# Turning the input rows on VectorE instead of TensorE, and two column groups of the query latent at once

## The reference, cut to what matters

```
h = rmsnorm(x) * norm_gain                    # over 4096 features
p = h @ w_in                                  # 4096 x about 14,000 columns
cq, ckv, kpe, mq, mk, mv, mo, mi, mf, za, zb = columns of p   # cq has 1536
y = x + [MLA(cq, ckv, kpe) * silu(za) ; mLSTM(mq, mk, mv, mo, mi, mf) * silu(zb)] @ w_out
```

## Time and profile before

| | us |
|---|---|
| median of 3 runs (lowest, highest) | 2008.21 (2006.99, 2009.09) |
| profiled execution | 2007.37 |
| its span | 2005.6 |
| TensorE busy in the span | 1996.1 |
| VectorE, ScalarE, GpSimd busy | 1191.9, 910.7, 192.3 |
| granted clock of TensorE, mean | 0.999 of full |

### The profile page before, as it was taken

How to read it: one execution, slowest core, us unless ns; L and a number is a source line. 1 busy time by engine, 2 the same in 40 slices (tenths; PEclk the granted TensorE clock), 3 DMA queues, 4 the chain that set the end, 5 groups by cost and what they waited for, 6 DMA issues and landing times.

```text
span 2005.6 us, 36262 instructions
## 1 busy us (share of the span) xinstructions
PE 1996.1 (100%) x14891; PEld 1972.6 (98%) x14891; DVE 1191.9 (59%) x2292; ACT 910.7 (45%) x1814; POOL 192.3 (10%) x228
## 2 busy tenths in 40 slices
PE   9999999999999999999999999999999999999998
PEld 9999999999999999999999999999999999999998
DVE  5545677776566576666765555444455665555544
ACT  5644456565444443334444444444444543333333
POOL 0011043434200000000000001000000000000000
PEclk9999999999999999999999999999999999999999
DMA  9655443333455454645546555555555566666665
GB/s 253 185 172 155 121 123 106 109 102 124 118 172 148 146 170 126 178 128 168 158 139 176 169 168 168 169 168 168 169 168 168 169 184 193 195 193 193 194 192 141
DMA packets 213821, 323.27 MB, mean 161 GB/s; under 512 B 25104, under 2 KB 89128, under 8 KB 213656
## 3 DMA queue, kind: packets, MB, share of 16 engines
q1 hardware_dynamic: 210408, 317.42, 54.8%
q10 hardware_dynamic: 3248, 3.54, 0.5%
HBM read 310.11 MB, written 9.62 MB: 159 GB/s over the span
## 4 chain that ended last, share of the span: by engine, by line
PE 99%; DMA 0%; DVE 0%; ACT 0%; issue 0%; ACTq 0%
PE bank L1769 30%; PE bank L1773 30%; PE bank L1772 30%; PE bank L2043 1%; PE bank L2013 1%; PE bank L1939 1%; PE bank L1942 1%; PE bank L1941 1%; PE bank L1794 0%; PE bank L2115 0%; PE bank L2141 0%; PE bank L2009 0%; PE bank L2010 0%; PE bank L2168 0%; PE bank L2153 0%; DMA con<-in_shape_table_dram 0%
## 5 line engine op out<-in xcount | busy, mean ns | idle before, releaser
L1154 DVE TENSOR_TENSOR wlo<-raw,whi 128x512 fp32r<-128x512 f32 (+1 forms) x1256 | 813.9, 658 | 744.4 <-ACT whi L753 739.5
L1769 PE MATMUL bank<-xsplit,whi 128*128 128x288 f32 (+2 forms) x4128 | 1221.1, 296 | 0.3 <-DVE wlo L1154 0.3
L1773 PE MATMUL bank<-xsplit,wlo 128*128 128x288 f32 (+2 forms) x4128 | 1213.3, 294 | 0.0
L1772 PE MATMUL bank<-xsplit,whi 128*128 128x288 f32 (+2 forms) x4128 | 1213.0, 294 | 0.0
L753 ACT CAST whi<-raw 128x512 fp32r<-128x512 f32 (+1 forms) x1256 | 707.1, 575 | 953.3 <-PE bank L1773 910.4
L1769 PEld LDWEIGHTS bank<-xsplit,whi 128*128 128x128 f32 (+1 forms) x4128 | 774.1, 188 | 3.3 <-DVE wlo L1154 1.2
L1772 PEld LDWEIGHTS bank<-xsplit,whi 128*128 128x128 f32 (+1 forms) x4128 | 774.1, 188 | 1.8 <-issue 1.0
L1773 PEld LDWEIGHTS bank<-xsplit,wlo 128*128 128x128 f32 (+1 forms) x4128 | 773.5, 187 | 0.0
L1769 PE MATMUL bank<-latents,whi 128*128 128x288 f32 (+1 forms) x352 | 112.8, 320 | 0.1
L1772 PE MATMUL bank<-latents,whi 128*128 128x288 f32 (+1 forms) x352 | 107.0, 304 | 0.0
L1773 PE MATMUL bank<-latents,wlo 128*128 128x288 f32 (+1 forms) x352 | 106.8, 303 | 0.0
(11 more groups left out here) (303 smaller groups left out, 1227.6 us busy)
## 6 DMA issues: line engine op xcount, KB each, us to landing
raw<-in_w_in_dram SPq DMA_DIRECT2D x313, 512.0 KB, 3.8
raw<-in_w_out_dram SPq DMA_DIRECT2D x128, 512.0 KB, 3.9
raw<-in_w_in_dram SPq DMA_DIRECT2D x146, 256.0 KB, 3.1
raw<-in_w_q_up_dram SPq DMA_DIRECT2D x48, 384.0 KB, 3.4
raw<-in_w_kv_up_dram SPq DMA_DIRECT2D x16, 512.0 KB, 3.7
xres<-in_x_prompt_dram SPq DMA_DIRECT2D x32, 128.0 KB, 3.8
out_dram<-ytok SPq DMA_DIRECT2D x28, 128.0 KB, 3.5
xt<-in_x_prompt_dram SPq DMA_DIRECT2D x7, 384.0 KB, 8.9
```

The source lines that it names most:

```text
L1154: ins = tt(lo, src, hi.bitcast(f32), ALU.subtract)
L1769: ins = mm(out, w_hi, m_hi, start=start, stop=False, **kw)
L1772: mm(out, w_hi, m_lo, start=False, stop=False, **kw)
L1773: return mm(out, w_lo, m_hi, start=False, stop=stop, **kw)
```

## The change

**x is loaded in another layout and turned by VectorE.** `xt` is now 4 quarters of 32 partitions; a quarter holds a quarter of the features of a chunk of k tiles, for all token rows, in 10 blocks of 32 rows (the first block: 16 zero rows and the 16 meta rows; 8 of the prompt; one of the sample). Chunks are of 2, 2, 4, 4, ... k tiles. VectorE's `transpose` turns every 32 by 32 square of [128, 10 x 32] at once, reading every second or fourth element. A k tile then holds the features m·p + j of its chunk on partition p, so the weight rows are loaded in that order (`w_rows`, `qk_rows`), and the gains are laid out so on the host. The loads of x are 4 DMAs of 32 partitions per chunk, with 512 B runs (256 B in the first two chunks); the sample and meta rows are 12 DMAs at chunk 0 and chunk 2.

**Two groups at once.** Groups 0 and 1 become one loop of 64 units: unit 2k is columns 0 to 511 of k tile k in banks 0 to 3, unit 2k + 1 columns 512 to 1023 in banks 4 to 7. A slot of `raw` holds the 1024 columns of one k tile in 4 KB runs. The third group is as before.

**Row sums.** Ten squares of [128, 1024], one at each step of the third group (12 at every second step before); one fp32 matmul of 304 columns in place of three. **Narrow units.** 18 DMAs in place of 8. **Tables.** The loads of the constants and of the cache move to the third group. **Warming.** 18 transposes in one go.

```diff
-X_BLOCKS = [(0, 256), (256, 512)] + [(a, a + 512) for a in range(512, D_MODEL, 512)]
+CHUNKS = [(0, 2), (2, 2)] + [(k, 4) for k in range(4, KT, 4)]
-WARM = (4, 9)
+WARM = 18
 @@ SyncE
+        def w_rows(k, n, cols):
+            k0, m = CHUNKS[chunk_of(k)]
+            return w_in[k0 * P:(k0 + m) * P, cols].rearrange("(p k) c -> p k c", k=m)[:, k - k0:k - k0 + n, :]
+        def x_rows(eng, b):
+            k0, m = CHUNKS[b]
+            w, at = SQUARE * m, SQUARE * k0
+            for a in range(4):
+                f = k0 * P + a * w
+                eng.dma_start(xt[SQUARE * a:SQUARE * a + SQUARE, 1:9, at:at + w],
+                              x_prompt[0, :, f:f + w].rearrange("(b r) e -> r b e", r=SQUARE)).then_inc(x_in[b], 16)
+        def x_end_rows(eng, b, n, rows, places):
...
+            for a in places:
+                eng.dma_start(xt[SQUARE * a + r0:SQUARE * a + SQUARE, block, at:at + n * w]
+                              .rearrange("r (n e) -> r n e", n=n), src[a]).then_inc(x_in[b], 16)
+            x_rows(sp, 0)
+            sp.wait_ge(eps_set, 2)
+            x_end_rows(sp, 0, 2, meta, (0, 1))
+            first_weights(0)
+            x_rows(sp, 1)
+            first_weights(1)
+            first_weights(2)
+            sp.wait_ge(eps_set, 3)
+            x_end_rows(sp, 2, len(CHUNKS) - 2, x_sample[0], range(4))
+            x_end_rows(sp, 2, len(CHUNKS) - 2, meta, range(4))
+            for k in range(3, KT):
+                if k % 4 == 3 and k < KT - 1:
+                    x_rows(sp, chunk_of(k + 1))
+                first_weights(k)
 @@ ScalarE
+        def first_groups(x_part, now, after):
+            for k in range(KT):
+                for u in (2 * k + AHEAD, 2 * k + AHEAD + 1):
+                    if u == 2 * k + AHEAD and k + X_AHEAD < KT:
+                        x_part(k + X_AHEAD)
+                    if u < 2 * KT:
+                        now(u)
+                    else:
+                        after(u - 2 * KT)
             def x_tile(k):
-                b = 4 + k % 4
-                act.wait_ge(full[b], use("x", b, k // 4) + 1)
-                nc.scalar.activation(xhi[:, k, :], bank[b][:, 0:NT], ACT.Copy,
+                act.wait_ge(x_turned, k + 1)
+                nc.scalar.activation(xhi[:, k, :], xs[:, k % 2, X_PAD:], ACT.Copy,
 @@ VectorE
+            def x_turn(k):
+                b = chunk_of(k)
+                k0, m = CHUNKS[b]
+                if k == k0:
+                    dve.wait_ge(x_in[b], 16 * X_PIECES[b])
+                if k >= 2:
+                    dve.wait_ge(xlo_d, k - 1)
+                at = SQUARE * k0
+                nc.vector.transpose(xs[:, k % 2, :].rearrange("p (b r) -> p b r", r=SQUARE),
+                                    xt[:, :, at + k - k0:at + SQUARE * m:m]).then_inc(x_turned, 1)
+            for k in range(KT):
+                if k + X_AHEAD < KT:
+                    x_turn(k + X_AHEAD)
+                for u in (2 * k + AHEAD, 2 * k + AHEAD + 1):
+                    if u < 2 * KT:
+                        two_units(u)
+                    else:
+                        cq_units(u - 2 * KT)
+                    if u == 2 * k + AHEAD and k + X_AHEAD < KT:
+                        x_rest(k + X_AHEAD)
 @@ TensorE
-            warm(WARM[0])
-            for k in range(X_AHEAD):
-                x_tile(k)
-            warm(WARM[1])
-            group(0, "cq", 0, 0, N_META, lambda k: x_tile(k + X_AHEAD) if k + X_AHEAD < KT else None, x_ready=True)
+            warm(WARM)
+            for k in range(KT):
+                pe.wait_ge(xlo_d, k + 1)
+                for half in range(2):
+                    u = 2 * k + half
+                    pe.wait_ge(lo_done, u + 1)
+                    for ct in range(4) if k else (0, 2, 1, 3):
+                        b, s = 4 * half + ct, slice(ct * P, ct * P + P)
+                        ins = mm3(bank[b][:, 0:NQ], ...)
...
-                    for t, (c0, n) in enumerate(X_TOK):
-                        ins = mm(bank[4][:, c0:c0 + n], ones[0:n, :], diag[0:n, c0:c0 + n], start=True, stop=True)
+                    mm(bank[4][:, 0:NT], ones, diag[:, X_PAD:], start=True, stop=True).then_inc(full[4], 1)
```

More of the change, by code:

```diff
@@ L161, in shape_constants @@
     part("gains")[:] = gain_columns(inputs)
-    part("perm")[0:112, :] = np.roll(np.eye(112, dtype=np.float32), N_META, axis=1)
+    part("squares")[:] = np.tile(np.eye(SQUARE, dtype=np.float32), (P // SQUARE, 1))
     for b in range(2):
@@ L197, in gain_columns @@
         t[:, at:at + len(rows)] = rows.T
+    rows = np.asarray(inputs["norm_gain"]).reshape(-1)
+    for k, m in CHUNKS:
+        t[:, G_X + k:G_X + k + m] = rows[k * P:(k + m) * P].reshape(P, m)
     for at, name in ((G_QR, "q_rope_norm"), (G_KR, "k_rope_norm")):
@@ L468, in load, with group @@
                 sp.dma_start(dst, src).then_inc(raw_in[slot], 16)
-            def group(b0, col, src=w_in_t, blocks=KT // 2, width=512, first=0, between=lambda n: None):
+            def group(b0, col, src=w_rows, blocks=KT // 2, width=512, first=0, between=lambda n: None):
                 for n in range(first, blocks):
@@ L516, in cache_rows @@
                 if n == 0:
-                    for b in range(4, 8):
-                        sp.wait_ge(full[b], use("cq", b))
+                    sp.wait_ge(xlo_d, KT)
                     sp.dma_start(cacher[:, 0:512], cache_ckv[0]).then_inc(cache_in, 16)
@@ L659, in _ @@
             for i in range(0, 8):
-                group(U_OUT // 2 + i * (KT // 2), i * 512, w_out_t, between=out_rows(i))
+                group(U_OUT // 2 + i * (KT // 2), i * 512, lambda k, n, cols: w_out_t[:, k:k + n, cols],
+                      between=out_rows(i))
             for half in range(2):
@@ L680, in hymba_step @@
         T_NAR = [4 * turns] * RAW_SLOTS
-        T_PAIR = [4 * turns + 2] * RAW_SLOTS
+        T_PAIR = [4 * turns + d for d in NAR_LOADS]
         T_ML = [t + MLA_HEADS // 2 * pair_turns for t in T_PAIR]
@@ L768, in x_tile, with cq_evict @@
                                      scale=G[:, G_X + k:G_X + k + 1]).then_inc(xhi_d, 1)
-            def cq_evict(i):
+            def cq_evict(phase, g, b0=0):
                 for ct in (0, 2):
[L773 to L777, removed]
-                    x_tile(k)
-                cq_units(0)(k)
@@ new lines, in cq_evict @@
+                    nc.scalar.copy(cqraw[:, ds(g * 4 + ct, 1), :], bank[b0 + ct][:, 0:NQ]).then_inc(free[b0 + ct], 1)
+            for k in range(X_AHEAD):
+                x_tile(k)
+                two_units(2 * k)
+                if 2 * k + 1 < AHEAD:
+                    two_units(2 * k + 1)
+            first_groups(x_tile, two_units, cq_units)
+            cq_evict("cq_two", 0)
+            cq_evict("cq_two", 1, 4)
+            def x_squares(k):
+                if k < X_ROWS:
+                    if k == 0:
+                        for b, pieces in enumerate(X_PIECES):
+                            act.wait_ge(x_in[b], 16 * pieces)
+                        act.wait_ge(eps_set, 3)
+                    else:
+                        act.wait_ge(xsq, k)
+                    nc.scalar.activation(junk[:, :], xt[:, k, :], ACT.Square, accum_out=xss[:, k:k + 1])\
+                        .then_inc(xsq, 1)
@@ L806, in _, with row_hooks, ckv_units @@
-            cq_evict(1)
-            steps(KT, cq_units(2), cq_units(3), row_rstd)
-            cq_evict(2)
+            def row_hooks(k):
+                x_squares(k)
+                row_rstd(k)
+            def ckv_units(k):
+                unit(U_CKV + k, k, landed(T_CKV, k))
+            steps(KT, cq_units, ckv_units, row_hooks)
+            cq_evict("cq", 2)
             def ckv_hooks(k):
@@ L829, in narrow_units @@
             def narrow_units(k):
-                unit(U_NAR + k, k, landed(T_NAR, k, 0, 2), 288)
+                unit(U_NAR + k, k, landed(T_NAR, k, 0, NAR_LOADS[k // 2]), 288)
             def pair_units(n):
@@ L835, in pair_units @@
                 return split
-            steps(KT, lambda k: unit(U_CKV + k, k, landed(T_CKV, k)), narrow_units, ckv_hooks)
+            steps(KT, ckv_units, narrow_units, ckv_hooks)
             def rstd(dst, src, scale, bank_no, used, done):
@@ new lines, in _ @@
+            for k in range(X_AHEAD):
+                x_turn(k)
+            for k in range(X_AHEAD):
+                x_rest(k)
+                two_units(2 * k)
+                if 2 * k + 1 < AHEAD:
+                    two_units(2 * k + 1)
+            for k in range(KT):
[8 more added lines that the diff above has]
+                        x_rest(k + X_AHEAD)
@@ L1189, in row_squares @@
+            cq_evict("cq_two", 0)
+            cq_evict("cq_two", 1, 4)
+            def row_squares(k):
+                if k == 11:
+                    dve.wait_ge(xsq, X_ROWS)
+                    for b in range(X_ROWS):
+                        ts_(diag[:, SQUARE * b:SQUARE * b + SQUARE], c("squares"), xss[:, b:b + 1], None,
```

(2 more changed lines are left out.)

224 lines of the change are left out of this document (93 added, 131 removed).

## The result

| us | before | after |
|---|---|---|
| median (lowest, highest; runs) | 2007.74 (2006.99, 2009.09; 4) | 2028.83 (2028.04, 2029.58; 4) |
| profiled execution, span | 2007.37, 2005.6 | 2029.58, 2027.8 |

The kernel got slower by 21.1 us: ratio 1.0107, 95% interval 1.0095 to 1.0119. The prediction said 2005.6 with a range to 2013.0; it was wrong.

A forecast was written before the change was run, and what follows sets the result against it. TensorE's work was taken to bound the kernel, with a VectorE-ScalarE chain pacing the double group: its end moves from 118.19 to 115.9 us, 2.3 saved, with row sums 2.6, giving 2005.6 us by the median; range 2000.0 to 2013.0.

The forecast's parts named there:

- row sums: On TensorE, one fp32 matmul of 304 columns replaces six records of 0.58 us: 0.3 us saved.
- TensorE's side: TensorE's list: 30 in-line x transposes gone, 9.2 us, plus row sums 0.3; worth 9.5 us if nothing else limited.
- what I cost at nothing: Squares, bank copies, ten more narrow-unit DMAs and weight row order: all hidden by leads and cover, so 0 us.
- the full slow turn: Turn at its upper end, 0.83 us: a double-group step of 3.60 us and 2014.5 us in all.
- I take 0.50, the nearest form in size and source.: VectorE's turn of 128 x 320 in the double group: 0.50 us, between bounds of 0.37 and 0.83.
- the chain: Double group: VectorE and ScalarE wait on each other, 3.27 us per k tile against TensorE's 3.12.
- the strided turn is slow: Rival: turn up to 0.83 us, step 3.60, 2014.5 us; slower than before beyond a 0.60 turn; chance 0.16.
- The other five terms: Double-group step besides the turn: ScalarE's start 0.03, x tile 0.43, cast 0.65, two VectorE rests 1.22, x rest 0.44.
- I take 19.3: Start: k tile 3's weights, behind 28 issues, issued near 15.4 us and landing at 19.3; VectorE waits 2.9 us.
- short runs are dear: Rival at the start: 256 and 512 B runs cost double, k tile 3 lands at 24.5, +5.2: 2010.8 us; chance 0.12.
- TensorE sets the pace: Rival in the double group: step under 3.12 us, group ends at 111.2, 7.3 us less, 2000.9; chance 0.17.

The follow-up runs named there:

- e1: Changed kernel with an unused 352-byte tile ahead of nraw, putting xsplit and the later tiles back at their old addresses: 2014.54 us, ratio 1.0037.
- e3: e1 with VectorE's turn reading 32 elements in a row instead of every fourth or second (wrong outputs, same cost): 2007.65 us, ratio 1.0002.
- e6: e5 with the sample and meta rows of chunks 3 to 9 loaded behind k tile 4's weights, in eight more DMAs: 2001.53 us, ratio 0.997.
- e5: e1 with each VectorE turn done a step earlier, in mid-step between a weight rest and the x rest: 2004.23 us, ratio 0.9985.
- e10: e1 with only the rows of x in xsplit moved 4 bytes later, from byte 62540 to 62544: 2044.58 us, ratio 1.0187.

## Why the prediction was wrong

Forecast -2.6, measured +21.1: 23.7 to explain. The runs give:

| term | us | from |
|---|---|---|
| place of the rows against the weights | 14.3 | after - e1, 2028.83 - 2014.54 (13.8 if each is taken against the kernel before measured beside it) |
| turn 0.745 in place of 0.50 | 7.0 | 27 steps x 0.26 (3.53 - 3.27); e1 - e3 measured 6.9 |
| weights of k tile 3 at 21.4, not 19.3 | 2.1 | the cast's row |
| sum | 23.4 | |

The last two terms can be seen at the start of the third group: 125.55 for 115.9 is 9.65 us, of which they make 9.1. The 0.3 us of the row sums was not measured by itself.

- *"TensorE's side"*, and "what I cost at nothing": the price of a matmul was taken as fixed, so that only a changed list could change TensorE's time. This failed, for 14.3 us of the 23.7. The table part of the change, smaller constants, was priced at nothing because no instruction went with it. No rival had it either. It carried the result far out of the range, but even without it, in e1, the time is 2014.5 and the range ended at 2013.0, short of the full slow turn that the prediction itself had priced at 2014.5.
- *"I take 0.50, the nearest form in size and source."* This is the failed term of the chain. The upper bound of 0.83 was the nearer end, and the rival *the strided turn is slow* came true: its point of decision was a turn of 0.60; with 0.745 its own sum is -2.6 + 27 x 0.26 = +4.4. The Trainium skill (SBUF — State Buffer, "Door 1: The DMA port swizzle") wants two hits for each 16-byte line for full bandwidth and gives 4 fp32 as the free step. The turns at step 2 (two hits a line, 0.50) agree; those at step 4 (one hit, 0.745: 22.9 us for all 32 turns, less four of 0.50, over 28) are not free: (745 - 500)/320 = 0.77 ns more an element. The measurement decides.
- The other five terms held within 0.02 us, and the step of e3 (3.29 against 3.27) confirms the sum. The turns start 0.61 after the start of a rest, as was said of turns that all start at partition 0.
- *"I take 19.3"* for k tile 3: the issue came 1.2 us earlier than computed (14.19 for 15.4: 0.48 us an issue, not 0.525), and the landing was later all the same, 7.2 us from issue to cast instead of 3.8. The row of issues was not what held it: e6 left the number of issues and took bytes and short runs away, and gained. In kind that is the rival *short runs are dear*, at 2.1 us of its 5.2; runs of 256 and 512 B are most of the packets there, and the comparison of e5 and e6 points to their length, but length and bytes were not varied apart. The clock's dip behind the wait (0.83 in the window from 20 to 30 us) was not in the sum; in e6 the landing is earlier and the dip is gone, and it is 2.7 us faster than e5 by the medians.
- *TensorE sets the pace*, 2000.9, is nearly what e6 reaches with 2001.53: 5.7 us less than the kernel before measured beside it, where the rival has 7.3, and the third group at 111.71, where it has 111.2. Most of the value of the change was there; the order of VectorE's list, what SyncE's queue carried ahead of k tile 3, and an address hid it.
- e1 stands 7.3 us over the kernel before, where the terms without the place give -2.6 + 7.0 + 2.1 = 6.5; the interval of its ratio is 4.6 to 10.0 us.

## What to carry to other kernels

When a change alters the size of any tile, compare the start addresses of what TensorE streams and of its weights before and after, and count the matmuls of an untouched stage in a window of full clock: 752 for 772 was an address here, and an unused tile gave them back. Try such a tile before you judge the edit. Price an engine's access pattern by a row with the same step, and where there is none let the range reach to the dear end of that term. When two engines hand a tile to and fro, write the chain of one step and look whether an instruction can move up a step in one list; e5 gained 10.3 us so, without removing any work.

## What was not expected of the hardware

- A 288-column fp32r matmul in a full row takes 0.1300 or up to 0.14 us with the same instructions, and moving the streamed rows relative to the weights changes it: 4 bytes cost 30 us here (e10 against e1). Of the seven differences tried only one, 45004 bytes, is fast in both late windows. Why that one, and why 44652 and 45132 are fast or nearly so in some stages, stays open.
- VectorE's 32 by 32 transposes of 128 x 320 fp32 take 0.50 us at steps of one and two elements and 0.745 at a step of four.
- After 2.9 us without work, TensorE ran at half its clock for about 2.8 us (granted clock 0.50 from 23 to 25 us, matmuls 0.24 apart).
